# Output projection of the middle mixer: two-pass fp32 matmuls replaced by three products of high and low fp32r parts

## Chip, cores, metric

One core of one Trainium2 chip runs the whole program, launched once. The metric is the device time of that core in microseconds (us), and smaller is better. The kernel before takes 2828.0 us, the median of three runs (2827.4 to 2834.32).

## The reference, cut to what matters

The program is two small networks in a row, each of two layers, with D = 1024 features and fp32 data throughout. The change is in layer 0 of the second network, whose mixer joins an attention output and the output of a recurrent scan and multiplies both by one 1024 x 1024 weight. It does so for 256 latent and 256 context tokens, 512 in all.

```
def even_mixer(h_lat, h_ctx, ..., w_out, ...):
    ...
    o_lat = jnp.concatenate([oa_lat, ob_lat], axis=-1) @ w_out
    o_ctx = jnp.concatenate([oa_ctx, ob_ctx], axis=-1) @ w_out if ctx_out else None

def second_block(...):
    ...
        x = x + m_lat[:, 5] * o_lat
        x = x + 0.5 * m_lat[:, 8] * swiglu(modulate(rms_norm_2(x), ...), ffn_in[l, 1], ffn_out[l, 1])
        if ctx_out:
            ctx = ctx + m_ctx[5] * o_ctx
```

## The kernel before, in words

The program is written engine by engine: `schedule` lists the stages, and each engine has its own function of every stage's name. Engines meet only at semaphores. `barrier` between stages is a meeting of TensorE, ScalarE and VectorE: none of the three goes on before all three have come.

**Data.** Features lie on the 128 partitions, in KC = 8 chunks; x, o and hn are 128 x 8 x 512 (TOK = 512 tokens). Every weight comes as a stream of 1 MB tiles, 1024 x 256 each, over SyncE's DMA queue into a ring of three slots (`ring`). A tile holds the weights of two output chunks, called halves here (m = 0 and 1). SyncE loads tile n once the semaphore `tile_used` says that tile n - 3 is done with. `take_tile` on TensorE waits for the last product of the tile before, reports it used and waits for the next; `release_tile` with `first(mm)` lets the next matmul report it instead.

**The stage in question, `project("w_out_2e", 0, TOK)`.** It stands after `readout` (which normalises the scan's output on VectorE and writes the last four chunks of o) and before the norm and the second feed-forward of that layer. For each of the eight output chunks c, TensorE makes 8 fp32 matmuls (128 x 128 weights from the ring, 128 x 512 of o) into one PSUM bank (L910). VectorE then adds the bank, times a gate, to x (`gated_add`, L2079), ScalarE squares the new x (`square`, L1520), and TensorE sums the squares over features with a matmul against ones (`sum_squares`, L876), two chunks at a time after chunks 3, 5 and 7 and two more at the end. The next norm uses that sum.

**How the feed-forwards and the mixers' input projections do it.** ScalarE copies a half's weights, 128 x 1024, to a buffer of type fp32r, which keeps the high part (`split_high`, L1532). VectorE subtracts that from the weights to get the low part (`split_low`, L1991). Activations are split the same way in the norm (L1572 and L2021). TensorE then makes three fp32r matmuls for each pair of chunks: high x high, high x low, low x high (L1199, L1202, L1206 in the feed-forward; L943, L946, L950 in `blend`, the input projection). There are SPLITS = 2 buffers of split weights. The split of half n waits until half n - 1 has made its second matmul (`w_used`), since then half n - 2 is done.

In the names of the trace, `mix_o` is o of this mixer, `mix_in_x_hi`, `mix_in_w_hi` and so on are the split buffers that `blend` used for the input projection and that lie unused here, `win_...` are the same of the other layer, `ffn_...` those of the feed-forward, `bank` a PSUM bank. PEld is TensorE's loading of weights. Each fp32 matmul of the program stands in the trace as two MATMUL and two LDWEIGHTS records (128 of each for the 64 matmuls of this stage), each fp32r matmul as one.

## Time and profile before

| what | value |
|---|---|
| median of three runs | 2828.0 us |
| profiled execution, its own time | 2829.54 us |
| its span, first to last instruction | 2827.8 us |
| mean granted TensorE clock | 0.951 |
| busy: TensorE matmul, weight load | 2536.1 us (90%), 2006.7 us (71%) |
| busy: VectorE, ScalarE | 1515.0 us (54%), 891.9 us (32%) |
| matmuls of the stage (L910, 128 x 512) | 128 records, 57.7 us |

The granted clock is the share of TensorE's full 2.4 GHz that its clock gate let through: 1.00 is 2.4 GHz and 0.50 is 1.2 GHz. Busy shares are means over stages with different limits, so the stage itself is what has to be read.

### The profile page before, as it was taken

Reading aid. Unit: us, or ns where it says so; the run is one execution under the profiler, and the core shown is the slowest. Engines: PE = TensorE matmul, PEld = TensorE weight load, DVE = VectorE, ACT = ScalarE, POOL = GpSimd, SP = SyncE. Lnnn points to the kernel's source line nnn. Section 1 sums busy time; section 2 is a strip of 40 time slices with the busy share of each in tenths; the row PEclk is TensorE's granted clock in tenths of the full one; section 3 lists DMA queues with packets and bytes.
Section 4 is the critical chain, followed back from the end, with each engine's and each line's share of the span. In section 5 each row is a group of like instructions: output and inputs, shape, how many; then the busy total and the mean of one; then the engine's idle time right before and its main releaser. Section 6 shows DMA issues by size and latency. Waiting matters only on the chain.

```text
span 2827.8 us, 41887 instructions
## 1 busy us (share of the span) xinstructions
PE 2536.1 (90%) x17518; PEld 2006.7 (71%) x17518; DVE 1515.0 (54%) x2517; ACT 891.9 (32%) x1547; POOL 76.5 (3%) x148
## 2 busy tenths in 40 slices
PE   8999999799997899548886899998999997888998
PEld 6687778588875567248773588876788875556998
DVE  5656475555554655674543555545555543664554
ACT  2331131422222333712220422223322223343543
POOL 0000000000000000000000000000000000000000
PEclk9999999999998999779998999999999998999999
DMA  7235436243433110000011243443344441101553
GB/s 285 82 118 200 172 121 220 99 142 135 148 134 136 60 45 31 0 2 4 4 39 52 84 147 137 141 149 119 129 139 142 142 143 69 43 30 45 175 184 134
DMA packets 55770, 309.72 MB, mean 110 GB/s; under 512 B 5920, under 2 KB 9376, under 8 KB 28064
## 3 DMA queue, kind: packets, MB, share of 16 engines
q1 hardware_dynamic: 32944, 224.74, 22.2%
q0 software_dynamic: 20736, 75.51, 8.0%
q10 hardware_dynamic: 1904, 6.80, 0.6%
q8 instruction: 140, 2.29, 0.3%
q14 instruction: 46, 0.38, 0.0%
HBM read 305.98 MB, written 1.05 MB: 109 GB/s over the span
## 4 chain that ended last, share of the span: by engine, by line
PEld 39%; PE 31%; issue 12%; DVE 11%; ACT 7%; DMA 1%; PEldq 0%; DVEq 0%; ACTq 0%; SPq 0%
PEld bank L1206 13%; PEld bank L1199 13%; PEld bank L1202 12%; PE bank L1079 4%; PE bank L1258 4%; PE bank L1076 2%; PE bank L1052 2%; PE bank L1138 2%; PE bank L1154 2%; PE bank L943 2%; PE bank L950 2%; PE bank L946 2%; ACT hn L1567 2%; PEld bank L910 1%; PE bank L1033 1%
## 5 line engine op out<-in xcount | busy, mean ns | idle before, releaser
L1991 DVE TENSOR_TENSOR w_lo<-ring,w_hi 128x1024 fp32r<-128x1024 f32 (+1 forms) x198 | 236.2, 1193 | 450.6 <-ACT w_hi L1532 450.6
L1202 PE MATMUL bank<-ffn_x_lo,w_hi 128*128 128x512 f32 x1008 | 399.6, 396 | 0.0
L1206 PE MATMUL bank<-ffn_x_hi,w_lo 128*128 128x512 f32 x1008 | 399.6, 396 | 0.0
L1199 PE MATMUL bank<-ffn_x_hi,w_hi 128*128 128x512 f32 x1008 | 399.6, 396 | 0.0
L1532 ACT ACTIVATE w_hi<-ring 128x1024 fp32r<-128x1024 f32 (+1 forms) x198 | 203.7, 1029 | 290.2 <-PE bank L1202 278.6
L1923 DVE SCALAR_TENSOR_TENSOR ms<-mod_rows,c_silu 128x1024 f32<-128x1024 f32 x200 | 243.9, 1220 | 1.2
L1206 PEld LDWEIGHTS bank<-ffn_x_hi,w_lo 128*128 128x128 f32 x1008 | 189.9, 188 | 46.3
L1199 PEld LDWEIGHTS bank<-ffn_x_hi,w_hi 128*128 128x128 f32 x1008 | 189.9, 188 | 46.3
L1202 PEld LDWEIGHTS bank<-ffn_x_lo,w_hi 128*128 128x128 f32 x1008 | 189.8, 188 | 46.3
L1199 PE MATMUL bank<-ffn_h_hi,w_hi 128*128 128x512 f32 x528 | 211.7, 401 | 0.0
L1206 PE MATMUL bank<-ffn_h_hi,w_lo 128*128 128x512 f32 x528 | 209.3, 396 | 0.0
L1202 PE MATMUL bank<-ffn_h_lo,w_hi 128*128 128x512 f32 x528 | 209.3, 396 | 0.0
L1079 PE MATMUL bank<-hn,ring 128*128 128x256 f32 x768 | 176.5, 384 | 3.4 <-PE bank L1079 3.1
L1079 PEld LDWEIGHTS bank<-hn,ring 128*128 128x128 f32 x768 | 144.9, 192 | 31.0 <-issue 12.9
L1199 PE MATMUL bank<-ffn_x_hi,ffn_h_hi 128*128 128x256 f32 (+1 forms) x400 | 125.3, 313 | 46.4 <-DVE ffn_x_lo L2021 46.4
L1761 ACT ACTIVATE ffn_h_hi<-rs 128x512 fp32r<-128x512 f32 (+1 forms) x88 | 50.9, 579 | 324.6 <-DVE rs L2293 324.6
L813 POOL DMA_DIRECT2D mod_rows<-in_mod_stream x144 | 76.3, 530 | 2237.2 <-DVEq L1926 1626.8
L1755 ACT ACTIVATE sq<-bank 128x512 f32<-128x512 f32 (+1 forms) x88 | 47.9, 544 | 237.0 <-PE bank L1206 236.9
L2001 DVE TENSOR_TENSOR ffn_h_lo<-ring,ffn_h_hi 128x1024 fp32r<-128x1024 f32 (+1 forms) x68 | 80.7, 1193 | 77.0 <-ACT ffn_h_hi L1540 77.0
L1199 PEld LDWEIGHTS bank<-ffn_x_hi,ffn_h_hi 128*128 128x128 f32 x400 | 78.7, 197 | 60.5 <-issue 40.1
L1202 PE MATMUL bank<-ffn_x_lo,ffn_h_hi 128*128 128x256 f32 (+1 forms) x400 | 121.6, 304 | 0.0
L1206 PE MATMUL bank<-ffn_x_hi,ffn_h_lo 128*128 128x256 f32 (+1 forms) x400 | 121.4, 304 | 0.0
(430 smaller groups left out, 4642.8 us busy)
## 6 DMA issues: line engine op xcount, KB each, us to landing
ring<-in_stream SPq DMA_DIRECT2D x211, 1024.0 KB, 4.8
mod_rows<-in_mod_stream POOLq DMA_DIRECT2D x144, 512.0 KB, 3.8
one_const<-in_one ACTq DMA_DIRECT2D x1, 1665.0 KB, 14.2
mix_const<-in_two ACTq DMA_DIRECT2D x1, 1440.0 KB, 6.2
win_const<-in_win ACTq DMA_DIRECT2D x1, 1089.0 KB, 5.4
x<-in_x SPq DMA_DIRECT2D x4, 256.0 KB, 4.5
c_silu<-in_c SPq DMA_DIRECT2D x1, 1024.0 KB, 10.3
x<-in_x SPq DMA_DIRECT2D x1, 1024.0 KB, 26.5
```

The source lines that it names most:

```text
L813: pool.dma_start(mod_rows[:, n % 2, :], ins["mod_stream"][n]).then_inc(sem(f"mod_rows_in{n % 2}"), 16)
L943: mm = pe.matmul(bank[:, :], high[:, kc, :], hi, start=kc == 0, stop=False)
L946: mm = pe.matmul(bank[:, :], high[:, kc, :], lo, start=False, stop=False)
L1079: mm = pe.matmul(bank[:, 0:SEQ], w[:, kc * COLS + m * P:kc * COLS + (m + 1) * P], hn[:, kc, 0:SEQ], start=kc == 0, stop=kc == KC - 1)
L1199: mm = pe.matmul(bank[:, 0:tok], w_high, hi, start=k == 0, stop=False)
L1202: mm = pe.matmul(bank[:, 0:tok], w_high, lo, start=False, stop=False)
L1206: mm = pe.matmul(bank[:, 0:tok], w_low, hi, start=False, stop=last)
L1258: mm = pe.matmul(part(bank[r, col]), lhs[r, col], part(rhs[r, col]), start=True, stop=True)
L1532: nc.scalar.activation(place(n)[0][:, 0:h.nk, :], raw_half(h), ACT.Copy).then_inc(sem("w_hi_ready"), 1)
L1923: link(V.scalar_tensor_tensor(products[:].rearrange("p a b -> p (a b)"), mod_rows[:, part // 2, :], 1.0, c_silu[:, part % 2, :], ALU.mult, ...
L1991: V.tensor_tensor(low[:, 0:h.nk, :], raw_half(h), high[:, 0:h.nk, :].bitcast(F32), ALU.subtract).then_inc(sem("w_split"), 1)
L2001: V.tensor_tensor(low[:, 0:h.nk // 2], raw_last(h), high[:, 0:h.nk // 2].bitcast(F32), ALU.subtract).then_inc(sem("w_split"), 1)
```

## The change

The stage has a function of its own, `project_parts`. It works as `blend` does: ScalarE and VectorE split the weights of each half and the eight chunks of o, and TensorE makes three fp32r products where it made one fp32 matmul. The product of low by low is left out. In the diff the three functions are those of TensorE, ScalarE and VectorE, in that order. The buffers are the ones that `blend` used; no tile, DMA or memory is added. The other mixer's projection (`project("w_out_2o", ...)`) stays as it is.

```diff
-    s["project"]("w_out_2e", 0, TOK)
+    s["project_parts"](TOK)
...
+def out_halves(order):
+    at = order.index(("w_out_2e", 0, 0))
+    return [Half("out", at + c // 2, c % 2, 0, KC, c) for c in range(KC)]
...
+            def project_parts(tok):
+                b_w, b_o = tally("w_split", KC), tally("o_split", KC)
+                for c, h in enumerate(parts_out):
+                    pe.wait_ge(sem("w_split"), b_w + c + 1)
+                    tile_no[0] = h.tile + 1
+                    if h.m == 1:
+                        release_tile()
+                    bank, full = take_bank()
+                    high, low = mixed_half(0)(c)
+                    for kc in range(KC):
+                        if c == 0:
+                            pe.wait_ge(sem("o_split"), b_o + kc + 1)
+                        hi, lo = ph2["x_hi"][:, kc, 0:tok], ph2["x_lo"][:, kc, 0:tok]
+                        mm = pe.matmul(bank[:, 0:tok], high[:, kc, :], hi, start=kc == 0, stop=False)
+                        if kc == 0:
+                            first(mm)
+                        mm = pe.matmul(bank[:, 0:tok], high[:, kc, :], lo, start=False, stop=False)
+                        if kc == 0 and c > 0:
+                            mm.then_inc(sem("w_used"), 1)
+                        mm = pe.matmul(bank[:, 0:tok], low[:, kc, :], hi, start=False, stop=kc == KC - 1)
+                    mm.then_inc(full, 1)
+                    if h.m == 1 and c > 1:
+                        sum_squares(c - 3, tok)
+                        sum_squares(c - 2, tok)
+                for c in (KC - 2, KC - 1):
+                    sum_squares(c, tok)
...
+            def project_parts(tok):
+                used = tally("w_used", KC - 1)
+                split_high(parts_out, 0, used, mixed_half(0), 0)
+                for kc in range(KC):
+                    nc.scalar.activation(ph2["x_hi"][:, kc, 0:tok], ph2["o"][:, kc, 0:tok], ACT.Copy).then_inc(sem("o_hi_ready"), 1)
+                split_high(parts_out, 1, used, mixed_half(0), 0)
+                came = []
+                for c in range(KC):
+                    if 2 <= c + 1 < KC:
+                        split_high(parts_out, c + 1, used, mixed_half(0), 0)
+                    if c == 4:
+                        turns.next()
+                    came.append(turns.next())
+                    if c:
+                        b, use = came[c - 1]
+                        act.wait_ge(bank_free[b], use + 1)
+                        square(c - 1, tok)
...
+            def project_parts(tok):
+                b_o = tally("o_hi_ready", KC)
+                split_low(parts_out, 0, mixed_half(0))
+                for kc in range(KC):
+                    dve.wait_ge(sem("o_hi_ready"), b_o + kc + 1)
+                    V.tensor_tensor(ph2["x_lo"][:, kc, 0:tok], ph2["o"][:, kc, 0:tok], ph2["x_hi"][:, kc, 0:tok].bitcast(F32),
+                                    ALU.subtract).then_inc(sem("o_split"), 1)
+                split_low(parts_out, 1, mixed_half(0))
+                for c in range(KC):
+                    if 2 <= c + 1 < KC:
+                        split_low(parts_out, c + 1, mixed_half(0))
+                    if c == 4:
+                        sums.append(turns.next())
+                    bank, free = full_bank()
+                    gated_add(bank, free, 0, 5, c, tok)
```

The instructions move on three engines. TensorE at the start of the stage, before the change: the last row of `readout`, then the stage, where the row with x7 stands for seven more matmuls of one chunk.

```order
L1402 MATMUL bank<-rec_lw,base 128x512 [waits y_squares,bank_free2]
L910 MATMUL bank<-mix_o,ring 128x512 [waits bank_free3,slot_loaded2,stage_done]
L910 MATMUL bank<-mix_o,ring 128x512 x7
L910 MATMUL bank<-mix_o,ring 128x512 [waits bank_free4]
L910 MATMUL bank<-mix_o,ring 128x512 x7
L910 MATMUL bank<-mix_o,ring 128x512 [waits bank_full4,bank_free5,slot_loaded0]
```

The same place of the changed kernel (its line numbers are those of the changed file): two chunks of o, and then the first matmuls of the second half.

```order
L1442 MATMUL bank<-rec_lw,base 128x512 [waits y_squares,bank_free2]
L948 MATMUL bank<-mix_in_x_hi,mix_in_w_hi 128x512 [waits bank_free3,o_split,w_split,stage_done]
L951 MATMUL bank<-mix_in_x_lo,mix_in_w_hi 128x512
L955 MATMUL bank<-mix_in_x_hi,mix_in_w_lo 128x512
L948 MATMUL bank<-mix_in_x_hi,mix_in_w_hi 128x512 [waits o_split]
...
L948 MATMUL bank<-mix_in_x_hi,mix_in_w_hi 128x512 [waits bank_free4,w_split]
L951 MATMUL bank<-mix_in_x_lo,mix_in_w_hi 128x512
L955 MATMUL bank<-mix_in_x_hi,mix_in_w_lo 128x512
```

The first matmul now waits for split weights and a split chunk of o as well, each of the first half's eight triples waits for its chunk, and the wait for the last bank (`bank_full4`) in front of each new tile is gone.

ScalarE in the same stage, before the change: from the last root of `readout` to the third square.

```order
L1514 ACTIVATE rs<-rs 128x512 [waits act_step]
L1520 ACTIVATE sq<-x 128x512 [waits bank_free3,stage_done]
L1520 ACTIVATE sq<-x 128x512 [waits bank_free4]
L1520 ACTIVATE rs<-x 128x512 [waits bank_free5]
```

ScalarE of the changed kernel, from the same root on.

```order
L1575 ACTIVATE rs<-rs 128x512 [waits act_step]
L1593 ACTIVATE mix_in_w_hi<-ring 128x1024 [waits slot_loaded2,stage_done]
L1499 ACTIVATE mix_in_x_hi<-mix_o 128x512 x8
L1593 ACTIVATE mix_in_w_hi<-ring 128x1024 [waits slot_loaded2]
L1593 ACTIVATE mix_in_w_hi<-ring 128x1024 [waits w_used,slot_loaded0]
L1581 ACTIVATE sq<-x 128x512 [waits bank_free3]
L1593 ACTIVATE mix_in_w_hi<-ring 128x1024 [waits w_used,slot_loaded0]
L1581 ACTIVATE sq<-x 128x512 [waits bank_free4]
```

Ahead of the squares stand the first two weight copies and the eight copies of o; after that each square has one weight copy in front of it.

VectorE of the changed kernel, from the last row of `readout` to the second gated add (two rows each); before the change only the rows of the gated adds (L2079 there) stood here.

```order
L2558 TENSOR_TENSOR mix_o<-hn,rec_g 128x512 [waits dve_step]
L2052 TENSOR_TENSOR mix_in_w_lo<-ring,mix_in_w_hi 128x1024 [waits dve_step,w_hi_ready,stage_done]
L2123 TENSOR_TENSOR mix_in_x_lo<-mix_o,mix_in_x_hi 128x512 [waits o_hi_ready] x8
L2052 TENSOR_TENSOR mix_in_w_lo<-ring,mix_in_w_hi 128x1024 [waits w_hi_ready]
L2156 SCALAR_TENSOR_TENSOR x<-bank,modv,x 128x256 [waits bank_full3]
L2156 SCALAR_TENSOR_TENSOR x<-bank,modv,x 128x256
L2052 TENSOR_TENSOR mix_in_w_lo<-ring,mix_in_w_hi 128x1024 [waits w_hi_ready]
L2156 SCALAR_TENSOR_TENSOR x<-bank,modv,x 128x256 [waits bank_full4]
```

The low part of the first half's weights stands ahead of the eight low parts of o, and that of the second half behind them.

## Rows read from the trace of the kernel before

**Rows 1.** The page: the span, and the chain that ended last.

```profile
span 2827.8 us, 41887 instructions
...
PEld 39%; PE 31%; issue 12%; DVE 11%; ACT 7%; DMA 1%; PEldq 0%; DVEq 0%; ACTq 0%; SPq 0%
```

**Rows 2.** Busy time by window: from:to, length, engines (records), clock, DMA share, GB/s.

```profile
1506.00:1567.00 61.00, 60.70 (x137) 26.64 (x138) 6.21 (x15) 4.41 (x7) 0.00 (x0) 0.97 0.15 52
1600.00:1700.00 100.00, 100.00 (x429) 80.39 (x428) 54.34 (x76) 28.22 (x36) 4.76 (x9) 1.00 0.40 140
```

**Rows 3.** Timeline, start of the stage: start us, length us, engine, line, operation, [idle before].

```profile
1505.01 0.69 DVE L2481 TENSOR_TENSOR mix_o<-hn,rec_g 128x512 f32<-128x512 f32 x1
1505.80 0.50 PEld L910 LDWEIGHTS bank<-mix_o,ring 128*128 128x128 f32 x2 [22.54 <-DVEq L2085]
...
1509.96 0.19 PEld L910 LDWEIGHTS bank<-mix_o,ring 128*128 128x128 f32 x1 [0.25 <-issue]
```

**Rows 4.** Timeline, end of the stage.

```profile
1565.87 0.19 PEld L910 LDWEIGHTS bank<-mix_o,ring 128*128 128x128 f32 x1 [0.24 <-issue]
1566.29 0.19 PEld L876 LDWEIGHTS bank<-sq,base 128*128 128x128 f32 x1 [0.24 <-issue]
...
1566.92 0.88 DVE L2079 SCALAR_TENSOR_TENSOR x<-bank,modv,x 128x256 f32<-128x256 f32 x2 [5.99 <-PE bank L910]
...
1567.83 0.63 ACT L1520 ACTIVATE rs<-x 128x512 f32<-128x512 f32 x1 [6.24 <-DVE x L2079]
```

**Rows 5.** Timeline, the first new tile within the stage.

```profile
1522.01 1.52 PE L910 MATMUL bank<-mix_o,ring 128*128 128x512 f32 x3 [0.30 <-PE bank L910]
```

**Rows 6.** Timeline, two fp32r halves in a row in `blend` of layer 1.

```profile
2395.63 0.19 PEld L943 LDWEIGHTS bank<-win_x_hi,win_w_hi 128*128 128x128 f32 x1
...
2396.54 1.05 ACT L1532 ACTIVATE win_w_hi<-ring 128x1024 fp32r<-128x1024 f32 x1
...
2397.62 1.23 DVE L1991 TENSOR_TENSOR win_w_lo<-ring,win_w_hi 128x1024 fp32r<-128x1024 f32 x1 [14.60 <-ACT win_w_hi L1532]
...
2401.11 0.19 PEld L943 LDWEIGHTS bank<-win_x_hi,win_w_hi 128*128 128x128 f32 x1
...
2406.32 0.19 PEld L950 LDWEIGHTS bank<-win_x_hi,win_w_lo 128*128 128x128 f32 x1
```

**Rows 7.** Timeline, the third half of the next feed-forward, and the fourth.

```profile
1596.61 0.19 PEld L1199 LDWEIGHTS bank<-ffn_x_hi,w_hi 128*128 128x128 f32 x1
...
1602.22 0.19 PEld L1199 LDWEIGHTS bank<-ffn_x_hi,w_hi 128*128 128x128 f32 x1
```

**Rows 8.** Timeline, the norm after the stage: from its barrier to the first fp32r matmul.

```profile
1570.40 2.00 ACT L1532 ACTIVATE ffn_h_hi<-ring 128x1024 fp32r<-128x1024 f32 x2 [1.94 <-PEq L996]
...
1571.49 1.23 DVE L1991 TENSOR_TENSOR ffn_h_lo<-ring,ffn_h_hi 128x1024 fp32r<-128x1024 f32 x1 [0.37 <-ACT ffn_h_hi L1532]
...
1578.74 0.69 DVE L2021 TENSOR_TENSOR ffn_x_lo<-hn,ffn_x_hi 128x512 fp32r<-128x512 f32 x1
...
1579.55 0.29 PEld L1199 LDWEIGHTS bank<-ffn_x_hi,ffn_h_hi 128*128 128x128 f32 x1 [10.06 <-issue]
```

**Rows 9.** Groups of instructions, window 1570 to 1600: count, busy us, mean ns, idle before.

```profile
L2021 DVE TENSOR_TENSOR ffn_x_lo<-hn,ffn_x_hi 128x512 fp32r<-128x512 f32 x8 | 5.5, 691 | 3.3 <-ACT ffn_x_hi L1572 3.3
...
L1572 ACT ACTIVATE ffn_x_hi<-hn 128x512 fp32r<-128x512 f32 x8 | 5.0, 631 | 0.3
```

**Rows 10.** Timeline of weight loads, the start of two feed-forwards.

```profile
513.50 0.28 PEld L1199 LDWEIGHTS bank<-ffn_x_hi,ffn_h_hi 128*128 128x128 f32 x1 [11.35 <-issue]
513.67 0.33 PEld L1202 LDWEIGHTS bank<-ffn_x_lo,ffn_h_hi 128*128 128x128 f32 x1
514.10 0.33 PEld L1206 LDWEIGHTS bank<-ffn_x_hi,ffn_h_lo 128*128 128x128 f32 x1
...
516.44 0.19 PEld L1202 LDWEIGHTS bank<-ffn_x_lo,ffn_h_hi 128*128 128x128 f32 x1
...
1585.64 0.19 PEld L1199 LDWEIGHTS bank<-ffn_x_hi,ffn_h_hi 128*128 128x128 f32 x1 [0.77 <-DVE ffn_x_lo L2021]
```

More of the change, by code:

```diff
@@ L338, in project @@
             order.append((name, 0, j))
+    def project_parts(tok):
+        for j in range(4):
+            order.append(("w_out_2e", 0, j))
     def mixer(layer):
@@ L363, in weight_order @@
              "rwkv_features decays wkv readout store").split()
-    schedule(dict(blend=blend, project=project, mixer=mixer, leave=leave, ffn=ffn, **{n: quiet for n in names}))
+    schedule(dict(blend=blend, project=project, project_parts=project_parts, mixer=mixer, leave=leave, ffn=ffn, **{n: quiet for n in names}))
     return order
@@ L523, in build @@
         parts_of = [blend_halves(order, layer) for layer in range(2)]
+        parts_out = out_halves(order)
         def split_half(n):
@@ L1408, in _ @@
             schedule(dict(
-                start=start, norm=norm_and_count, blend=blend, project=project, mixer=mixer, leave=leave,
+                start=start, norm=norm_and_count, blend=blend, project=project, project_parts=project_parts, mixer=mixer, leave=leave,
                 barrier=barrier, ffn=ffn, load_two=load_two, load_window=load_window,
@@ L1453, in project @@
                     square(c, tok)
+            def project_parts(tok):
[15 more added lines that the diff above has]
+                        square(c - 1, tok)
+                b, use = came[KC - 1]
+                act.wait_ge(bank_free[b], use + 1)
+                square(KC - 1, tok)
             def blend(layer):
@@ L1886, in _ @@
             schedule(dict(
-                start=start, norm=norm_counted, blend=blend, project=project, mixer=mixer, leave=leave,
+                start=start, norm=norm_counted, blend=blend, project=project, project_parts=project_parts, mixer=mixer, leave=leave,
                 barrier=barrier, ffn=ffn, load_two=load_two, load_window=load_window,
@@ L2055, in project, with project_parts @@
                     gated_add(bank, free, layer, 5, c, tok)
+            def project_parts(tok):
+                b_o = tally("o_hi_ready", KC)
[12 more added lines that the diff above has]
+                    gated_add(bank, free, 0, 5, c, tok)
             def blend(layer):
@@ L2484, in _ @@
             schedule(dict(
-                start=start, norm=norm, blend=blend, project=project, mixer=mixer, leave=leave,
+                start=start, norm=norm, blend=blend, project=project, project_parts=project_parts, mixer=mixer, leave=leave,
                 barrier=barrier, ffn=ffn, load_two=load_two, load_window=load_window,
```

## Prediction

> **What bounds the kernel now.** I read the page first: the chain that ended last is 39% weight loads and 31% matmuls, so TensorE's stream is the time, and work of another engine matters only where TensorE waits for it [rows 1]. Second, the busy times by window: over the stage (1506 to 1567) TensorE is busy 60.70 of 61 us, at a granted clock of 0.97, while VectorE has 6.21 us of work and ScalarE 4.41 [rows 2]. So this stage is bound by TensorE alone, both other engines are nearly free to split, and an instruction saved on TensorE is time saved. Third, the timeline at both ends of the stage. TensorE's first weight load of the stage is at 1505.80, right after VectorE's last write of o [rows 3]. Its last is at 1565.87, and the sums of squares that close the stage begin at 1566.29 [rows 4]. What I replace is therefore the stretch from 1505.80 to 1566.29, **60.49 us**. Everything after it (gated add, last square, last sums, barrier, norm) has the same instructions in both kernels.
>
> **What a matmul costs before.** At full clock one record follows another at 0.43 us: the last load of the stage and the next are 1565.87 and 1566.29 [rows 4]. More exactly: from 1509.96 on there are 122 records of the projection and 8 of the four sums between them, 130 in 56.33 us, with one pause of about half a us where `take_tile` waits for the last bank (the row at 1522.01 shows 0.30 of it as idle) [rows 3, 4, 5]. (56.33 - 0.54)/130 = 0.429 us. An fp32 matmul is two records, 0.858 us, and a half of eight is 6.87 us.
>
> **What it costs after.** A half is 24 fp32r matmuls. In `blend` a half begins at 2395.63 and the next at 2401.11, so 5.48 us or 0.2283 each; the next one's 24 loads span 2401.11 to 2406.32, 23 steps of 0.2265 [rows 6]. In the feed-forward a half takes 1602.22 - 1596.61 = 5.61 us [rows 7]. Nothing tells me what makes that difference of 2%. I take 5.48, because the stage uses the same kind of buffers as `blend`, and keep 5.44 and 5.62 as ends. Saved per half: 6.87 - 5.48 = 1.39 us.
>
> The Trainium skill (FP8 and Floating Point Precision, section TensorE Precision Notes) says that true FP32 takes four passes through the array. The row agrees: 0.858 us is 3.76 times the 0.2283 of one fp32r matmul. By that rule alone three passes for four would save a quarter of the stream, and by the rows it is 20%, because an fp32r matmul takes a little longer than half an fp32 record.
>
> **The first half, term by term.** Times are from the point where TensorE started before, 1505.80.
> - Wait for the splits. All three engines leave the barrier together. ScalarE copies the first weights: two such copies took 2.00 us, and VectorE began its subtraction 1.09 us after the first copy began, for 1.23 us [rows 8]. That ends at 2.32. Then VectorE makes the first low part of o, 0.69 us with 0.03 between instructions [rows 9], to 3.04. ScalarE's copy of that chunk (1.0 + 0.63 us) is ready long before. From a low part's end (1578.74 + 0.69) to TensorE's load at 1579.55 are 0.12 us [rows 8]. TensorE starts at **3.15 us**. This term is new and nothing hides it; it is the price of the change.
> - Half clock. TensorE has been idle for over 20 us and the granted clock is at 1.2 GHz when it starts. Before, loads come slowly until 1509.96, 4.16 us after the start [rows 3]. Elsewhere this lasts 2.9 us (513.50 to 516.44) and up to 6.1 (1579.55 to 1585.64) [rows 8, 10]. At half clock fp32r matmuls follow at 0.43 us (513.67 to 514.10) [rows 10], so 4.16 us make (4.16 - 0.13)/0.43 = 9.4 matmuls, the first being 0.13 slower; the other 14.6 take 3.34 at full clock. The half takes **7.5 us** (6.9 with 2.9 us of half clock, 8.4 with 6.1). The term hardly changes the difference, since before as well half of that time was lost.
> - VectorE feeds a chunk per 0.72 us, and TensorE uses one in 3 x 0.43 = 1.29 us, later 0.685. It does not catch up: the last chunk is there at 2.32 + 8 x 0.72 = 8.1 us, TensorE reaches it at about 10.
>
> **The other seven halves.** 7 x 5.48 = **38.4 us**, if each finds its split weights. For half c + 1 ScalarE starts its copy once half c has made its second matmul (0.4 us), takes 1.05, VectorE 1.23 (the same pair ran from 2396.54 to 2398.85, and the next half began at 2401.11, 2.26 us later) [rows 6]. ScalarE has a square (0.63) and VectorE a gated add (0.88) per half besides [rows 4]: 1.7 and 2.1 us of 5.48. The second half's weights are the tightest. Their low part stands behind eight low parts of o: 8.1 + 1.23 = 9.3, and the first half ends at 3.15 + 7.5 = 10.65, so 1.3 us are left. The pause at a new tile is gone, since nothing waits for a bank any more.
>
> The four sums between the halves stay: 8 x 0.429 = **3.43 us**.
>
> **Sum.** 3.15 + 7.5 + 38.4 + 3.43 = 52.5 us against 60.49: **8.0 us less**. The tile releases come earlier (with the second half of a tile, no longer after it), so the next tiles are never later. The profiled execution took 2829.54 us for a span of 2827.8; by the sum it would be 2821.5. The median of the runs shown is 1.5 lower, so I forecast **2820.0 us**. I take 0.3% (8.5 us) as what a measurement can tell from no change, and the forecast lies just inside it.
>
> **The rivals.**
> - *A faster stream.* For: an fp32 record makes two passes of 512 columns in 0.429, so a pass is 0.215 us; if an fp32r matmul took just that, a half would be 5.15 us. Seven halves would save 2.3 us more and the first one 0.2: 10.5 less, 2817.5. Against: the closest pace in rows is 0.2265 [rows 6], in every buffer. Chance 0.08. The Trainium skill's TensorE: Matmul & The Clock Gate, section Back-to-back issue gap, gives N/2.4 + 2.5 ns, which is 216 ns for 512 columns. By that the time is this rival's; the rows of this kernel have 227 to 234.
> - *A dearer entry.* If the splits of o came slower than I take them (ScalarE and VectorE at once on the same chunks is not in the trace, VectorE's last stands 1.3 us ahead of need) or the wait for the second half showed, I would lose 1 to 4 us more: about 2823. Against: in the norm the same two engines alternate at 0.69 and 0.63 [rows 9]. Chance 0.11.
> - *The weight splits are exposed.* If the chain of copy and subtraction did not run under the half before it, TensorE would wait for it six times. Its price is 0.4 + 1.05 + 1.23 = 2.7 us, and with a square and a gated add queued ahead of it 4.2: 6 x 4.2 = 25 us, less the 8 saved, so 17 slower, 2845. It decides from 8.0/6 = 1.3 us of exposed wait per half. For: ScalarE's queue is strict, and each square there waits for VectorE's gated add, which stands behind a subtraction. Against: the copy for half c + 1 stands ahead of the square of c - 1, whose add needs only the half before, and 2.26 us are left over in the rows with the same chain [rows 6]. Chance 0.04.
>
> **How the numbers follow.** My forecast has 0.77. Its own range is 7.0 to 9.0 us less: 5.62 per half gives 7.0, 5.44 gives 8.3, and a half-clock stretch shorter by a us in one kernel than in the other moves it by 0.5. With a spread between runs of 1.5 us this is 2818 to 2822. The range over all cases, 2816.5 to 2824.5, takes in the faster stream and the dearer entry and leaves the exposed splits out. Of my forecast 0.4 lies beyond 8.5 us: 0.31, and with the faster stream 0.39 for faster. Slower is the last rival, 0.04. Within 0.3% is the rest, 0.57.
>
> **What the changed kernel's profile would show.** TensorE's first load of the stage comes about 3.2 us after VectorE's last write of o. The first half has gaps only at its start, and takes 7 to 8 us. Seven halves are 5.4 to 5.6 us each with no idle before their first matmul. VectorE's idle in front of its subtractions, released by ScalarE, stays, as that costs nothing. The stage is about 8 us shorter and all later stages are as long as before. The prediction is wrong if TensorE shows waits for split weights in halves 1 to 7, if its pace is not between 0.226 and 0.235, or if a later stage, such as the start of the next feed-forward, gives back what this one gains.

## The result, and the profile after

The changed kernel takes 2817.3 us (median of 5 runs, 2811.98 to 2820.83) beside 2828.14 us of the kernel before (median of 5). The ratio is 0.995, with a 95% interval of 0.9936 to 0.9964: 10 to 18 us less. Forecast were 2820.0 us and a range of 2816.5 to 2824.5. The new median lies in that range, but the kernel before was given as 2828.0, so the forecast meant 8 us less, and the change measured is larger than that.

The page of the changed kernel, for [rows 1]:

```profile
span 2819.1 us, 42055 instructions
...
PEld 40%; PE 30%; issue 11%; DVE 11%; ACT 7%; DMA 1%; PEldq 0%; DVEq 0%; ACTq 0%; SPq 0%
```

The chain is made up nearly as before, each share within a point or so. The span, of one execution each, is 8.7 us shorter.

The timeline of the stage, for [rows 3] and [rows 4] (L948, L951 and L955 are the three matmuls of a triple, L1593 and L2052 the two weight splits, L1499 and L2123 those of o, L887 the sums):

```profile
1510.16 0.69 DVE L2558 TENSOR_TENSOR mix_o<-hn,rec_g 128x512 f32<-128x512 f32 x1
1510.93 1.06 ACT L1593 ACTIVATE mix_in_w_hi<-ring 128x1024 fp32r<-128x1024 f32 x1 [8.69 <-DVEq L2162]
1511.89 4.26 ACT L1499 ACTIVATE mix_in_x_hi<-mix_o 128x512 fp32r<-128x512 f32 x8
1512.09 1.23 DVE L2052 TENSOR_TENSOR mix_in_w_lo<-ring,mix_in_w_hi 128x1024 fp32r<-128x1024 f32 x1 [1.25 <-ACT mix_in_w_hi L1593]
1513.24 4.90 DVE L2123 TENSOR_TENSOR mix_in_x_lo<-mix_o,mix_in_x_hi 128x512 fp32r<-128x512 f32 x8
1514.04 0.29 PEld L948 LDWEIGHTS bank<-mix_in_x_hi,mix_in_w_hi 128*128 128x128 f32 x1 [25.63 <-issue]
...
1521.39 0.19 PEld L948 LDWEIGHTS bank<-mix_in_x_hi,mix_in_w_hi 128*128 128x128 f32 x1
...
1522.32 1.06 ACT L1593 ACTIVATE mix_in_w_hi<-ring 128x1024 fp32r<-128x1024 f32 x1 [5.23 <-PE bank L951]
...
1523.41 1.23 DVE L2052 TENSOR_TENSOR mix_in_w_lo<-ring,mix_in_w_hi 128x1024 fp32r<-128x1024 f32 x1 [0.73 <-ACT mix_in_w_hi L1593]
...
1526.83 0.19 PEld L948 LDWEIGHTS bank<-mix_in_x_hi,mix_in_w_hi 128*128 128x128 f32 x1
...
1532.27 0.19 PEld L948 LDWEIGHTS bank<-mix_in_x_hi,mix_in_w_hi 128*128 128x128 f32 x1
...
1563.00 0.42 PEld L887 LDWEIGHTS bank<-sq,base 128*128 128x128 f32 x2
1563.42 0.88 DVE L2156 SCALAR_TENSOR_TENSOR x<-bank,modv,x 128x256 f32<-128x256 f32 x2 [4.57 <-PE bank L955]
```

Read it as the prediction's sum. ScalarE leaves the barrier at 1510.93, which is where TensorE would have started, and TensorE's first load is 3.11 us later. The first half ends at 1521.39, 7.35 us on. The next two halves take 5.44 us each, and their first loads have no bracket, so nothing was waited for. The split for the half after ends at 1523.41 + 1.23 = 1524.64, 2.2 us ahead of its use at 1526.83. From the last write of o (1510.85) to the last sums are 52.15 us; before, they were 60.59 (1505.70 to 1566.29). So the stage gives **8.4 us**, and 8.6 up to the end of its last gated add (62.1 to 53.5), which is the measure of the stage from here on.

Three long stretches of the trace account for the rest, by window. First the changed kernel: the stage, the stretch from the scan to the last write of o, the window attention (from VectorE's first subtraction of split weights in layer 1's `blend` to the first gated add of the projection behind it), and 10 us near that stage's start.

```profile
1510.90:1563.00 52.10, 48.93 (x200) 38.94 (x200) 20.67 (x30) 16.29 (x23) 0.00 (x0) 0.93 0.23 81
1240.50:1510.90 270.40, 212.97 (x6876) 201.38 (x6866) 140.47 (x284) 61.83 (x111) 1.06 (x2) 0.86 0.04 15
2361.10:2573.40 212.30, 179.04 (x790) 118.11 (x791) 128.53 (x283) 94.00 (x239) 0.00 (x0) 0.92 0.09 30
2376.10:2386.10 10.00, 9.15 (x30) 6.74 (x31) 1.39 (x2) 2.97 (x6) 0.00 (x0) 0.71 0.01 2
```

And the kernel before, without the stage [rows 2]:

```profile
1240.60:1505.70 265.10, 206.34 (x6880) 193.77 (x6868) 140.37 (x284) 61.83 (x111) 1.05 (x2) 0.90 0.05 15
2364.90:2582.40 217.50, 184.47 (x790) 122.07 (x791) 128.61 (x284) 94.07 (x239) 0.00 (x0) 0.89 0.09 30
2379.90:2389.90 10.00, 9.15 (x27) 6.65 (x28) 1.38 (x2) 2.93 (x6) 0.00 (x0) 0.65 0.00 0
```

VectorE does 20.7 us of work in the stage where [rows 2] had 6.21, and TensorE's pace does not show it. The instructions of the other two stretches are the same in both kernels, and yet the scan took 5.3 us longer and the window attention 5.2 us less, each time with the granted clock: 0.86 against 0.90, and 0.92 against 0.89. All else agrees to 0.3 us but for the part before the scan's window, which gained and lost 1.6 at most. So the 8.7 us between these two traces are 8.6 of the change, and two clock effects of 5 us that cancel, in these two traces by chance. Over many runs they need not cancel. That is the question for the experiments.

### The profile page after: what moved, and what is told of

It reads as the page before. It is cut to its first block, busy times and chain, and to the rows that moved or that the text cites. A ratio compares the mean times of both kernels' runs of the same rounds, so it can differ in the third digit from the quotient of the medians.

```text
span 2819.1 us, 42055 instructions
## 1 busy us (share of the span) xinstructions
PE 2527.8 (90%) x17582; PEld 2023.7 (72%) x17582; DVE 1529.4 (54%) x2533; ACT 903.9 (32%) x1563; POOL 76.5 (3%) x148
## 4 chain that ended last, share of the span: by engine, by line
PEld 40%; PE 30%; issue 11%; DVE 11%; ACT 7%; DMA 1%; PEldq 0%; DVEq 0%; ACTq 0%; SPq 0%
PEld bank L1246 13%; PEld bank L1239 13%; PEld bank L1242 12%; PE bank L1119 4%; PE bank L1298 4%; PE bank L1116 2%; PE bank L1178 2%; PE bank L1194 2%; PE bank L1092 2%; PE bank L983 2%; PE bank L990 2%; PE bank L986 2%; ACT hn L1628 2%; PE bank L1073 1%; DVE stats L2206 1%
## 5 line engine op out<-in xcount | busy, mean ns | idle before, releaser
L2052 DVE TENSOR_TENSOR w_lo<-ring,w_hi 128x1024 fp32r<-128x1024 f32 (+1 forms) x198 | 236.2, 1193 | 450.7 <-ACT w_hi L1593 450.6
L1593 ACT ACTIVATE w_hi<-ring 128x1024 fp32r<-128x1024 f32 (+1 forms) x198 | 203.7, 1029 | 289.9 <-PE bank L1242 278.6
L1119 PEld LDWEIGHTS bank<-hn,ring 128*128 128x128 f32 x768 | 145.6, 193 | 31.3 <-issue 12.9
L1822 ACT ACTIVATE ffn_h_hi<-rs 128x512 fp32r<-128x512 f32 (+1 forms) x88 | 50.9, 579 | 324.6 <-DVE rs L2370 324.6
L1984 DVE SCALAR_TENSOR_TENSOR one_products<-mod_rows,c_silu 128x1024 f32<-128x1024 f32 x88 | 107.6, 1223 | 28.7 <-DMA mod_rows<-in_mod_stream 24.4
```

The lines of the kernel that those rows point to most:

```text
L1119: mm = pe.matmul(bank[:, 0:SEQ], w[:, kc * COLS + m * P:kc * COLS + (m + 1) * P], hn[:, kc, 0:SEQ], start=kc == 0, stop=kc == KC - 1)
L1593: nc.scalar.activation(place(n)[0][:, 0:h.nk, :], raw_half(h), ACT.Copy).then_inc(sem("w_hi_ready"), 1)
L1984: link(V.scalar_tensor_tensor(products[:].rearrange("p a b -> p (a b)"), mod_rows[:, part // 2, :], 1.0, c_silu[:, part % 2, :], ALU.mult, ...
L2052: V.tensor_tensor(low[:, 0:h.nk, :], raw_half(h), high[:, 0:h.nk, :].bitcast(F32), ALU.subtract).then_inc(sem("w_split"), 1)
```

## Experiments

Theory: the stage is worth 8.4 us as summed, and the rest of the measured gain is the granted clock elsewhere. Rivals: the sum's terms are wrong in ways that cancel; or the changed stage makes a later stage shorter by something that it leaves behind.

**The two kernels again (no edit).** First with timed runs:

> The kernel before, unchanged, to see how far runs of one program lie apart and where. Theory A (the change is worth the 8.5 us or so that the stage got shorter; what the medians show beyond that is where half-clock stretches of TensorE happen to fall in the scan and in the window attention): ratio 1.000 within 0.2%, single runs spread over 5 us or more, and the trace differs from the first one by several us in the scan (from 1240 us on) and in the window attention (2400 to 2560), with no instruction added. Theory B (the changed kernel is faster in later stages as well): the runs of this program agree within 2 us, and its trace agrees with the first one everywhere within 1 us.

> The changed kernel, unchanged, a second trace and five more runs. Both theories: the stage takes 52.1 us again from the barrier to the last sums. Theory A: the ratio comes out near 0.997 (8.5 us of 2829), and the trace differs from the first one of this kernel by several us in the scan and the window attention. Theory B: 0.995 again (14 us), with the window attention again 4 to 5 us shorter than before.

Measured: 2827.87 us (11 runs) for the kernel before, beside 2829.48 (17 runs) of its other runs, ratio 0.9994 [0.9983, 1.0006]; 2816.33 us (6 runs) for the changed one, 0.9957 [0.9944, 0.997], 8 to 16 us less. In the traces the stage takes 62.2 and 53.5 us up to its last gated add, the window attention 218.0 and 212.2. Then one more trace of each:

> The kernel before once more, for its trace. So far the window attention of layer 1 (from the norm's first subtraction of window weights to the first gated add of its projection) took 217.5 and 218.0 us in both traces of it and 212.2 in both of the changed kernel, where the first half-clock stretch of that stage ends later after its start in the slow ones. If the length belongs to the kernel: 217.5 to 218 again. If it is drawn anew in each run: 212.2 is as likely.

> The changed kernel once more, for its trace. The stage itself 53.5 us between the same marks as before (both traces so far). Window attention 212.2 again if its length belongs to the kernel, 217 to 220 possible if it is drawn anew.

Measured: 2828.49 us with a stage of 61.6 and a window attention of 217.4, and 2820.03 us with 54.3 and 217.4. The windows of the changed kernel's third trace (the stage; the window attention; 10 us near its start):

```profile
1504.40:1558.70 54.30, 51.06 (x203) 40.30 (x204) 21.56 (x33) 16.29 (x23) 0.00 (x0) 0.91 0.22 78
2355.30:2572.70 217.40, 184.27 (x790) 121.92 (x791) 128.64 (x284) 94.13 (x239) 0.00 (x0) 0.89 0.08 30
2370.30:2380.30 10.00, 9.15 (x27) 6.63 (x28) 1.38 (x2) 2.99 (x6) 0.00 (x0) 0.65 0.01 2
```

So the short window attention is no fixed property of the changed kernel: the same kernel also gives the length of before, with a clock of 0.89 and 0.65 in the same places as before.

**As much less work, without the change.** `cut_ten` is the kernel before with 10 of the projection's 64 matmuls left out (chunk 7 in six halves, chunks 6 and 7 in two).

```diff
-                    for kc in range(KC):
+                    nk = KC if layer else (6 if c >= 6 else 7)
+                    for kc in range(nk):
```

> The kernel before with 10 of the stage's 64 fp32 matmuls left out (the last chunk of o for every output chunk, the last two for the last two), so 10 x 0.858 = 8.6 us less on TensorE with no fp32r and no split. Theory A: the whole program is shorter by 8.6 us, ratio 0.997, the same as the changed kernel within the spread. Theory B, if the gain in later stages came from fp32r or the splits: 0.997 here but 0.995 for the changed kernel; if it came from the shift of time alone, 0.995 in both.

Measured: 2818.15 us (6 runs), 0.9962 [0.9948, 0.9976]. The stage takes 53.5 us, 8.6 less, and the window attention 212.2. Ten matmuls at 0.858 are 8.6 us, and the medians differ by 11.3, in a kernel with no split and no fp32r matmul in it. The interval, 7 to 15 us less, holds the 8.6 as well, so the timed runs alone do not show a further gain here. The trace shows that a short window attention can come without the new form of the projection. It is one trace, and whether the shorter stage brought it is a further question, taken up below.

**The entry.** `splits_fp32` makes and waits for all the splits, but multiplies in fp32 from the ring.

```diff
-                        mm = pe.matmul(bank[:, 0:tok], high[:, kc, :], hi, start=kc == 0, stop=False)
...
+                        mm = pe.matmul(bank[:, 0:tok], w[:, kc * COLS + m * P:kc * COLS + (m + 1) * P],
+                                       ph2["o"][:, kc, 0:tok], start=kc == 0, stop=kc == KC - 1)
```

> One part alone: all splits are made and waited for as in the changed kernel, but TensorE makes the old fp32 matmuls from the ring. The entry term alone should show: TensorE starts 3.15 us after VectorE's last write of o, and the stage takes 60.5 + 3.1 us. ScalarE's and VectorE's splits should cost nothing beyond that (1.7 and 2.1 us of work in 6.9 per half). If the splits themselves slowed TensorE (its reads of the ring against theirs), the pace of 0.429 us would rise.

Measured: 2831.66 us (10 runs), 1.001 [0.9998, 1.0022]. The stage is 66.1 us, 4.0 longer than before. Its timeline, the first load and the first short one:

```profile
1507.54 0.50 PEld L946 LDWEIGHTS bank<-mix_o,ring 128*128 128x128 f32 x2 [25.65 <-issue]
...
1513.47 0.19 PEld L946 LDWEIGHTS bank<-mix_o,ring 128*128 128x128 f32 x1 [0.31 <-issue]
```

TensorE starts 3.19 us after o's last write (1504.35), and the clock rises 5.9 us later, where [rows 3] had 4.2. Entry and longer half clock together are the 4.0. The pace behind is 0.43 per record as before, so splits made beside it cost TensorE nothing.

`early_splits` takes the entry away: the first half's weights, o's first chunk and three more high parts are split during `readout`. The low part of chunk kc goes to another place of its buffer, since the readout still reads the first ones.

```diff
             def readout():
+                split_high(parts_out, 0, 0, mixed_half(0), 0)
+                o_high(0)
...
+                    if m == 1:
+                        for kc in range(1, 4):
+                            o_high(kc)
```

> The changed kernel with the first half's weights and chunk 0 of o split in the stage ahead, where ScalarE is idle and VectorE waits, and the high parts of chunks 1 to 3 there as well. The entry term of 3.15 us should fall to about 0.1; VectorE's subtraction of weights ahead of the readout should cost about 0.8 there and the low part of chunk 0 about 0.1. Both theories: about 2 us less than the changed kernel between the scan's end and the last sums. If TensorE's half clock hid part of the entry, less than 1.

Measured: 2813.64 us (5 runs), 0.9948 [0.9936, 0.9961]: the fastest up to here, 15 us below before. Timeline of the entry:

```profile
1504.07 0.69 DVE L2569 TENSOR_TENSOR mix_o<-hn,rec_g 128x512 f32<-128x512 f32 x1
1504.85 2.19 ACT L1496 ACTIVATE mix_in_x_hi<-mix_o 128x512 fp32r<-128x512 f32 x4 [8.69 <-DVEq L2170]
1504.86 0.29 PEld L948 LDWEIGHTS bank<-mix_in_x_hi,mix_in_w_hi 128*128 128x128 f32 x1 [23.11 <-DVEq L2170]
```

TensorE starts 0.10 us after o's last write for 3.19 before, and the stage takes 50.7 us for 53.5. It gives 2.8 and not the full 3.1, since the first half takes 7.66 for 7.35: the clock rises 4.9 us after TensorE's start, for 4.2. The timed runs do not resolve these 2.8 us, as the interval overlaps both of the changed kernel's.

**Whether the weight splits hide.** `used_late` reports a half's buffer used after its 21st matmul, not its second, so that the split for the next half starts late.

```diff
-                        if kc == 0 and c > 0:
-
-                            mm.then_inc(sem("w_used"), 1)
                         mm = pe.matmul(bank[:, 0:tok], low[:, kc, :], hi, start=False, stop=kc == KC - 1)
+                        if kc == 6 and c > 0:
+                            mm.then_inc(sem("w_used"), 1)
```

> The changed kernel, but a half's buffer is reported used only after 21 of the next half's 24 matmuls, so that the split of the weights has 0.7 us of cover where it had 5. If the splits were hidden in the changed kernel only by that cover, each of halves 2 to 7 waits about 1.05 + 1.23 + 0.15 - 0.7 = 1.7 us, the stage is 10 us longer than in the changed kernel and the gain over the kernel before is gone. If they were not what hid, nothing changes.

Measured: 2829.46 us (10 runs), 1.0001 [0.9989, 1.0013]: the whole gain is gone. The stage takes 65.3 us, 3.2 more than before, and the time is the same as before; in its trace the window attention took 212.5. Timeline, from one copy to the half that needs it:

```profile
1514.99 1.06 ACT L1592 ACTIVATE mix_in_w_hi<-ring 128x1024 fp32r<-128x1024 f32 x1 [8.90 <-PE bank L952]
...
1516.08 1.23 DVE L2051 TENSOR_TENSOR mix_in_w_lo<-ring,mix_in_w_hi 128x1024 fp32r<-128x1024 f32 x1 [5.03 <-ACT mix_in_w_hi L1592]
...
1517.36 0.19 PEld L948 LDWEIGHTS bank<-mix_in_x_hi,mix_in_w_hi 128*128 128x128 f32 x1 [2.21 <-DVE mix_in_w_lo L2051]
```

This is what an exposed split looks like: TensorE's load carries a bracket with VectorE's subtraction as its releaser, 2.21 us, and a half takes 7.5 us for 5.44. Six such waits are the 12 us by which the stage is longer than the changed kernel's. In the changed kernel's trace no such bracket stands in front of any half after the first.

`one_product` leaves out two of the three products (high weights by high o alone), so that TensorE has only 8 matmuls per half to hide a split behind.

```diff
-                        mm = pe.matmul(bank[:, 0:tok], high[:, kc, :], lo, start=False, stop=False)
...
-                        mm = pe.matmul(bank[:, 0:tok], low[:, kc, :], hi, start=False, stop=kc == KC - 1)
```

> The changed kernel with high x high alone (8 matmuls per half; the products with the low parts are left out, all splits are still made and waited for). If the pace of 0.2266 us is TensorE's own, a half needs 1.8 us, and the chain of copy, subtraction and signals (0.45 + 1.05 + 1.23 + 0.15 = 2.9 us) becomes the bound: halves 1 to 7 follow at 2.9 us. This gives the length of half below which the splits show.

Measured: 2799.53 us (one run), a stage of 32.2. Timeline:

```profile
1520.86 1.70 PEld L948 LDWEIGHTS bank<-mix_in_x_hi,mix_in_w_hi 128*128 128x128 f32 x8 [1.52 <-DVE mix_in_w_lo L2049]
...
1521.98 1.06 ACT L1590 ACTIVATE mix_in_w_hi<-ring 128x1024 fp32r<-128x1024 f32 x1 [1.92 <-PE bank L948]
...
1523.07 1.23 DVE L2049 TENSOR_TENSOR mix_in_w_lo<-ring,mix_in_w_hi 128x1024 fp32r<-128x1024 f32 x1 [1.48 <-ACT mix_in_w_hi L1590]
...
1524.35 1.77 PEld L948 LDWEIGHTS bank<-mix_in_x_hi,mix_in_w_hi 128*128 128x128 f32 x8 [0.47 <-DVE mix_in_w_lo L2049]
```

Now the chain sets the pace: used, copy, subtraction, 3.3 to 3.7 us from half to half, where 2.9 were expected. A half with all three products has 5.44, so about 2 us are to spare, as [rows 6] let one expect. The prediction put the chain at 2.7. It took the copy to start 0.4 us after the half does; here it is 1.1, with the end of the second matmul as its releaser, in the changed kernel 0.93 (1521.39 to 1522.32), and [rows 6] already had 0.91 (2395.63 to 2396.54).

**The pace, by buffer.** `other_buffers` keeps the split weights in the feed-forwards' `w_hi` and `w_lo`.

```diff
-                    high, low = mixed_half(0)(c)
+                    high, low = w_hi[:, c % SPLITS], w_lo[:, c % SPLITS]
```

> The changed kernel with the split weights in the feed-forward's two buffers instead of the mixer's. If the place of the weights decides the pace, a half takes 5.62 us as in the feed-forward, not 5.44; if the activations or the stage decide, it stays 5.44.

Measured: 2819.92 us (one run). The starts of the second, third and fourth half:

```profile
1519.54 0.19 PEld L951 LDWEIGHTS bank<-mix_in_x_hi,w_hi 128*128 128x128 f32 x1
...
1525.16 0.19 PEld L951 LDWEIGHTS bank<-mix_in_x_hi,w_hi 128*128 128x128 f32 x1
...
1530.78 0.19 PEld L951 LDWEIGHTS bank<-mix_in_x_hi,w_hi 128*128 128x128 f32 x1
```

That is 5.62 us per half, the feed-forward's pace of [rows 7] to the hundredth, with nothing changed but where the weights lie. So the two paces that the prediction had to choose between, 0.2266 and 0.2342 us per matmul, go with the weights' buffers.

**What sets the window attention.** Its length goes with the time from its start to the rise of TensorE's granted clock some 20 us into it, which shows in the loads as well (0.50 us for a pair at half clock, 0.30 at full). All twenty traces, those of the runs below included, in the order of that time (all in us):

| trace | stage of the projection | start to rise | window attention |
|---|---|---|---|
| `other_buffers` | 55.6 | 20.7 | 212.1 |
| changed kernel, first and second; `cut_ten` | 53.5 | 20.8 | 212.2 to 212.3 |
| `early_splits` | 50.7 | 20.9 | 212.3 |
| `used_late` | 65.3 | 21.1 | 212.5 |
| `warm_early` | 50.9 | 21.4 | 212.7 |
| `delay_4` | 52.8 | 21.6 | 212.9 |
| kernel before: its three traces, three shifted forms, `warm_before` | 61.6 to 62.4 | 21.8 to 22.6 | 217.3 to 218.0 |
| `warm_after` | 54.3 | 21.9 | 213.1 |
| changed kernel, third | 54.3 | 21.9 | 217.4 |
| `delay_2` | 53.4 | 23.1 | 219.2 |
| `one_product` | 32.2 | 23.4 | 219.2 |
| `splits_fp32` | 66.1 | 23.4 | 219.5 |

So a shorter stage is neither needed for the short form nor enough for it: `used_late` has a longer stage than the kernel before and the short form, and `one_product`, with the shortest stage of all, has the long one.

Where the difference arises is in the traces too. VectorE's 201st instruction of the window attention starts 167.9 us into it in the changed kernel's first trace and 168.8 in that of the kernel before; the other 4.3 of the 5.2 us come after it. Two windows of 40 us that begin 159 us after the start, the changed kernel first:

```profile
2520.00:2560.00 40.00, 34.14 (x169) 19.64 (x168) 31.12 (x78) 20.42 (x61) 0.00 (x0) 1.00 0.05 20
2524.00:2564.00 40.00, 34.94 (x149) 20.66 (x147) 27.37 (x69) 17.55 (x53) 0.00 (x0) 0.87 0.06 24
```

In the short form the clock stays at full from there to the end. In all the others it falls to half again in this last part, so that the part's mean is 0.88 to 0.91.

`delay_2` and `delay_4` are the changed kernel with two and four extra VectorE copies behind the wait for the window constants.

```diff
                 dve.wait_ge(sem("window_in"), 16)
+                for k in range(2):
+                    link(V.tensor_copy(tmp[:, :], rstd[:, :]))
```

> The changed kernel with two idle VectorE copies of 128 x 512 (some 0.5 us each) ahead of the norm of layer 1's mixer. If the window attention's length is set by when TensorE's start falls against the rise of its granted clock, one us later changes the stretch from its start to the rise (14.0 us so far in the fast traces, 15.2 in those of 217.5 us, 16.6 in those of 219.5) and with it the length; if that length belongs to the change of the earlier stage, it stays 212.2 and the program is only the delay longer.

> The same with four copies, about 2.2 us. By the clock theory the start falls where it fell in the kernel before or nearby: window attention 217 to 220 us, and the program 7 to 10 us longer than the changed kernel for a delay of 2. By the other theory 2 us longer.

Measured: 2822.83 us (10 runs, 2813.27 to 2827.49), 0.997 [0.9956, 0.9984], and 2820.1 us (6 runs; a seventh took 3320.89 and is left out), 0.9964 [0.9951, 0.9978]. The copies are 1.0 and 1.9 us of work. The medians lie 5.5 to 6.5 and 3 to 4 us above those of the changed kernel, but the intervals of all of them overlap, so the runs show only that four copies cost no more than two. Windows of `delay_2`:

```profile
2362.20:2581.40 219.20, 186.78 (x790) 123.20 (x791) 128.59 (x283) 94.11 (x239) 0.00 (x0) 0.89 0.08 29
2377.20:2387.20 10.00, 9.15 (x24) 6.50 (x25) 1.39 (x2) 2.56 (x6) 0.00 (x0) 0.60 0.01 2
```

219.2 us, where `delay_4` has 212.9 and not the 217 to 220 that the clock theory gave. So between these single traces the same instructions differ by 6 to 7 us, up with a us of shift and down with another. The draws within one kernel (as between its second and third trace) are of the same size, so two traces don't fix the relation.

`warm_before` and `warm_after` are the two kernels with 14 extra matmuls, their result overwritten, in TensorE's idle time ahead of this stage, and `warm_early` the same for `early_splits`.

```diff
             def load_window():
+                b, use = turns.n % BANKS, turns.n // BANKS
+                pe.wait_ge(bank_free[b], use)
+                for k in range(14):
+                    pe.matmul(psum[b][:, :], ones, x[:, k % KC, 0:TOK], start=True, stop=True)
```

> The kernel before, with 14 extra fp32 matmuls of 512 columns (results overwritten) that TensorE makes in its idle 13.7 us ahead of layer 1's mixer (the window attention's stage), so that it does not enter that stage at half clock. Theory 'clock draw': the window attention's length in a run is set by the half-clock stretch at its start (212, 217.4 or 219.5 us); with TensorE warm that draw is gone, the stage is 212 us or a few less in both warm kernels, this kernel takes 2816 to 2822, and it is 8 to 9.5 us slower than the changed kernel with the same extra matmuls. Rival 'other cause': the 3 to 5 us by which the timed difference exceeds the stage's 8.5 lie elsewhere (the scan, or something the change does later); then both warm kernels move alike and their medians still differ by 12 to 14.

> The changed kernel with the same 14 extra matmuls. Clock draw: 2808 to 2813, 8 to 9.5 us below the warm kernel before, with window attention of the same length (within 1 us) in both traces, and a smaller spread between runs. Other cause: 12 to 14 us below the warm kernel before.

> The version with the first half's weights and the first chunk of o split in the readout, with the same 14 extra matmuls: the two improvements add up if they are independent, 2 us below the changed kernel with extra matmuls (the earlier stage was 2.8 shorter and its readout 0.9 longer): 2806 to 2811, below both kernels.

Measured: 2829.9 us (11 runs), 0.9996 [0.9988, 1.0005]; 2817.02 us (5 runs), 0.9951 [0.9938, 0.9964]; 2811.31 us (5 runs), 0.9933 [0.9913, 0.9953]. Windows of `warm_before`: the extra matmuls, the 10 us behind them, the window attention, and 10 us near its start.

```profile
2354.00:2366.00 12.00, 11.74 (x28) 4.97 (x27) 5.78 (x8) 4.66 (x6) 0.00 (x0) 1.00 0.27 93
2366.00:2376.00 10.00, 5.62 (x15) 2.26 (x14) 7.26 (x12) 9.78 (x20) 0.00 (x0) 0.85 0.00 0
2360.80:2578.70 217.90, 189.29 (x806) 123.94 (x805) 128.60 (x284) 94.10 (x239) 0.00 (x0) 0.92 0.09 30
2375.80:2385.80 10.00, 9.16 (x26) 6.60 (x27) 1.38 (x2) 2.88 (x6) 0.00 (x0) 0.63 0.00 0
```

The edit did not do what it was for. TensorE enters at full clock, but then it is busy for 5.6 of 10 us, feeding on chunks as VectorE makes them, and the clock falls and rises again where it always rose. The window attention takes 217.9 and 213.1 us, and the two still differ by 12.9. My theory as put (that a warm entry takes the draw away) is refuted, and the two traces have 7.7 of it in the stage (62.0 and 54.3) and 4.8 in the window attention. Their whole spans differ by 8.3 only, since all up to the last write of o took 3.8 us longer in `warm_after`.

Last, shifts of the kernel before. In `before_delay_2` and `before_delay_5` the copies stand ahead of the wait for the window constants, in `before_shift_2` two stand behind it.

```diff
             def load_window():
+                for k in range(5):
+                    link(V.tensor_copy(tmp[:, :], rstd[:, :]))
                 dve.wait_ge(sem("window_in"), 16)
```

> The kernel before with two extra VectorE copies ahead of the window attention, 1.0 us of added work on the path. Theory 'where the clock's rise falls': over all traces the attention takes 212 to 213 us where TensorE's clock rises 20.7 to 21.9 us after VectorE's first weight subtraction of that stage, 217.4 to 218 where it rises 21.9 to 22.6 after it, 219.2 to 219.5 at 23.1 to 23.4, and the moments of the rise do not move with the stage, so a start 1.0 us later meets a rise 20.9 to 21.6 us after it. Then this kernel, with more work, is faster than the kernel before: attention 212 to 213, 2825 to 2826 us, ratio 0.998 to 0.999. Rival (the shorter attention comes from something the changed stage leaves behind): attention stays at 217.5 and the time is 2830, 1 us slower.

> The same with five copies, 2.4 us of added work. Where the clock's rise falls: the next rise in reach is 22.9 to 23.6 us after the start, attention 218 to 219.5, 2832 to 2834 us, 6 to 9 us slower than with two copies for 1.4 us more work. Rival: 2831.5, attention 217.5.

Measured: 2830.74 us, 0.9998 [0.9988, 1.0007], and 2829.97 us, 0.9999 [0.9989, 1.0009], with window attentions of 217.9 and 217.8. They test nothing, as VectorE's timeline of `before_delay_5` shows:

```profile
2360.45 2.27 DVE L2315 COPY tmp<-rstd 128x512 f32<-128x512 f32 x5 [2.60 <-PEq L996]
2365.46 0.69 DVE L1969 TENSOR_SCALAR ms<-bank 128x512 f32<-128x512 f32 x1 [2.74 <-DMA win_const<-in_win]
```

The five copies ended 2.7 us before the constants landed, and hid there.

> The kernel before with two extra VectorE copies behind its wait for the window constants, where nothing hides them: the window attention starts 0.9 to 1.0 us later. Theory 'where the clock's rise falls': the rise that came 21.9 to 22.6 us after the start comes 20.9 to 21.7 us after it, the attention takes 212 to 213 us for 217.5, and the kernel with more work is faster, 2825 to 2826 us, ratio 0.998 to 0.999. Rival (the shorter attention comes from something the changed stage leaves behind): attention 217.5, time 2831, ratio 1.000 to 1.001.

Measured: 2829.46 us (11 runs), 0.9995 [0.9985, 1.0005], in its trace a window attention of 217.3 us:

```profile
2363.80:2581.10 217.30, 184.21 (x790) 121.90 (x791) 128.60 (x284) 94.16 (x239) 0.00 (x0) 0.89 0.09 30
2378.80:2388.80 10.00, 9.16 (x27) 6.64 (x28) 1.38 (x2) 2.97 (x6) 0.00 (x0) 0.66 0.00 0
```

The start did come 0.9 us later (399.2 us after the feed-forward's start, for 398.2 to 398.7), and the loads turned short 21.8 us after it, at the edge of the two groups: the shift of the clock's rise that the run was made for (to 20.9 to 21.7) did not come about in its trace. It confirms neither: the time is 4 us above what my theory gave and 1.5 below the rival's. `warm_after`, with the same clock of 0.66 in those 10 us, took 213.1.

## Why the prediction was wrong, step by step

- *The entry, "TensorE starts at 3.15 us"*: right, 3.11 after ScalarE's start and 3.19 after o's last write. VectorE's eight low parts took 4.90 us and not 8 x 0.72 = 5.8, so the tight second half had more time than I gave it.
- *"The half takes 7.5 us"*: 7.35.
- *"7 x 5.48 = 38.4" and the four sums of 3.43*: together 41.61 (1521.39 to 1563.00), for 41.8. The pace is 5.44, the lower of the ends kept, and `other_buffers` shows with which buffers the slower one, 5.62, goes. The rival's line "0.2265, in every buffer" was wrong by my own [rows 7], which give 0.234.
- *No exposed weight split*: right, with 2.2 us to spare, though the chain is 3.3 us and more where I had 2.7. `used_late` shows what losing them costs: 12 us, the whole gain.
- *"52.5 us against 60.49: 8.0 us less"*: 52.1, 8.4 less. The dearer entry, the faster stream and the exposed splits did not come. The Trainium skill's TensorE: Matmul & The Clock Gate, Back-to-back issue gap, gives 216 ns at 512 columns for the isolated gap. The traces have 227 and 234, with a weight load for each matmul.
- ***"All later stages are as long as before"* is the step that failed.** In the changed kernel the window attention, 800 us behind the change, took 212.3, 212.2, 217.4 and (with extra matmuls) 213.1 us, 213.8 on average; in the kernel before, with its three shifted forms and the one with extra matmuls, 217.3 to 218.0 in all seven traces, 217.7 on average. The stage is 53.9 and 62.1 us on average in the same traces. So 8.2 us of the stage and 3.9 of the window attention make 12.1 of the 13 that separate the medians (2829.5 and 2816.3, 2829.9 and 2817.0). The mechanism of the sum was right; the forecast put at nothing a term of about 4 us, and gave no reason but that the instructions of the later stages are the same. No rival had a later stage that becomes shorter.
- *"With a spread between runs of 1.5 us"*: 5 to 17 us between the fastest and the slowest run in every group of ten or more. The three runs first shown lay within 7 us, with two of them 0.6 apart, and I took those two for the spread. Beside the window attention it is the scan, 263.1 to 270.4 us in these traces with the same instructions.

Shown is that the window attention is about 4 us shorter on average in the changed kernel's traces, that this goes with the granted clock in it, above all in its last 50 us, that a kernel without the new matmuls can have the short form too (`cut_ten`), and that the length changes by 5 us between traces of one and the same kernel. That the change brings this gain by shifting the stage's start against the clock is argued from these and not shown: the one run that was to shift the kernel before towards the short form did not get it, and `used_late` and `one_product` show that the stage's length alone does not decide. What decides at the edge stays open, and so does how often each kernel draws the short form.

The best version measured is `warm_early`, 2811.31 us, 0.9933 [0.9913, 0.9953], with a window attention of 212.7. Its interval overlaps that of `early_splits`, and each is from 5 runs. I would keep `early_splits`, since nothing shows that the extra matmuls bring anything.

## What to carry to other kernels

Price a change by its own stage, and then ask which later stages run at a mixed clock: where TensorE is idle part of the time, the same instructions can take 212, 217 or 219 us from one run or kernel to the next, so a change far ahead of it can gain or lose as much again. Compare such stages over several traces of each kernel before the sum is trusted as the whole effect, and take the spread from all runs, not from the two that agree. Splitting fp32 weights into high and low parts pays when the chain of used, copy and subtraction (3.3 to 3.7 us here) fits beneath the half that covers it, and the first split is better made in the stage before where that has room (2.8 us of the stage here, by `early_splits`).

## What the runs showed of the hardware

- Three fp32r matmuls of 512 columns take 0.68 us at full clock with the weights in one pair of buffers and 0.70 in another, in the same stage (`other_buffers`, one run, for the latter); an fp32 one takes 0.858. Nothing here tells what about the buffers does it.
- TensorE that entered a stage at full clock fell to half in it, busy for 5.6 us of 10 (`warm_before`); and the clock then rose 22.5 us after the stage's start, no earlier than after an entry at half clock (21.8 to 22.6 in the other six traces of the kernel before and its forms).
- The same instructions of the window attention took 212 to 213 us in nine traces, 217.3 to 218.0 in eight and 219.2 to 219.5 in three. In the nine the clock stayed at full over the last 50 us; in the others its mean there was 0.88 to 0.91.
- A stage of 265 us (scan to last write of o) varied by 7.3 us between traces with the same instructions in it, with a granted clock from 0.86 to 0.90 in the two that are shown.
